# Triangular inversion in a WKV-7 scan: two of three chunk groups keep one factor in the other head's rows, and their products are issued beside those on the diagonal

## The reference, cut to what matters

```
def step(S, inp):
    r_t, w_t, k_t, v_t, a_t, b_t = inp
    sa = jnp.einsum('bhij,bhj->bhi', S, a_t)
    S = S * w_t[:, :, None, :] + sa[..., None] * b_t[:, :, None, :] + v_t[..., None] * k_t[:, :, None, :]
    return S, jnp.einsum('bhij,bhj->bhi', S, r_t)
```

## Time and profile before

| | |
|---|---|
| median of 3 runs | 2486.48 us (2485.86 to 2487.64) |
| the profiled execution | 2485.72 us, its span 2482.9 us |
| busy share of the span | TensorE 88%, VectorE 54%, GpSimd 48%, ScalarE 34% |
| stage B | 546 to some 1135 us |
| the pass looked at | G and N from 787 us, W(0) at 794.80, A at 820.79, next pass's G at 822.20 |

### The profile page before, as it was taken

One profiled execution on the slowest core, in us unless ns is written; L12 is line 12 of the kernel. 1 busy time (PEld: TensorE's weight loads), 2 busy tenths in 40 slices (PEclk: granted clock), 3 DMA queues, 4 the chain that ended last, 5 costly groups with the idle time before them and its releaser, 6 DMA issues.

```text
span 2482.9 us, 57378 instructions
## 1 busy us (share of the span) xinstructions
PE 2190.2 (88%) x22614; PEld 1847.4 (74%) x22614; DVE 1329.2 (54%) x1932; ACT 838.6 (34%) x2187; POOL 1201.1 (48%) x708
## 2 busy tenths in 40 slices
PE   6799999989999999986948989999894999798876
PEld 4698999888888888876948947777693876565655
DVE  6766666664665566655264314454316082548645
ACT  1623323335566656553021223323202111212331
POOL 1266666552233223318847802231583897775234
PEclk8899999999999999996969999999896999899998
DMA  2233334355234323422201210100121221121001
GB/s 88 87 136 145 137 144 166 143 174 96 65 70 88 88 64 69 88 90 78 93 34 69 93 51 35 34 17 34 35 92 71 99 87 43 60 76 60 18 0 68
DMA packets 158909, 197.61 MB, mean 80 GB/s; under 512 B 120992, under 2 KB 123296, under 8 KB 156448
## 3 DMA queue, kind: packets, MB, share of 16 engines
q1 hardware_dynamic: 158752, 195.25, 25.2%
HBM read 156.24 MB, written 38.99 MB: 79 GB/s over the span
## 4 chain that ended last, share of the span: by engine, by line
PE 55%; DVE 8%; issue 7%; ACT 4%; POOL 3%; DVEq 0%; ACTq 0%; POOLq 0%
PE wide L803 8%; PE wide L1233 8%; PE wide L1234 8%; PE wide L1235 8%; PE wide L1710 5%; PE wide L1819 2%; PE wide L818 2%; PE wide L1595 1%; PE wide L1775 1%; PE wide L1803 1%; PE wide L826 1%; PE wide L820 1%; PE wide L2072 1%; POOL x_w L1092 1%; DVE normed L1371 1%
## 5 line engine op out<-in xcount | busy, mean ns | idle before, releaser
L1233 PE MATMUL wide<-mixed_high,w_high_rwkv_in 128*128 128x264 f32 x720 | 212.2, 295 | 29.0 <-ACT log_decay L435 20.1
L1092 POOL TENSOR_TENSOR x_w<-n,masks 128x192 f32<-128x192 f32 x48 | 28.7, 599 | 381.5 <-ACT n L969 381.5
L1235 PE MATMUL wide<-mixed_high,w_low_rwkv_in 128*128 128x264 f32 x720 | 206.6, 287 | 0.0
L1234 PE MATMUL wide<-u_low_second,w_high 128*128 128x512 f32 x464 | 185.5, 400 | 0.0
L1257 POOL TENSOR_TENSOR w_high<-weights,con 128x1024 fp32r<-128x1024 f32 x60 | 147.5, 2458 | 73.7 <-PE wide L1235 63.8
L1350 DVE TENSOR_TENSOR sq_sum<-sq_sum,squares 128x528 f32<-128x528 f32 (+1 forms) x54 | 87.3, 1617 | 178.3 <-ACT squares L1315 178.3
L355 PE MATMUL wide<-mixed_in,weights 128*128 128x264 f32 x672 | 159.1, 395 | 13.3 <-DVE mixed_in L325 12.3
L1233 PEld LDWEIGHTS wide<-mixed_high,w_high_rwkv_in 128*128 128x128 f32 x720 | 138.2, 192 | 37.1 <-ACT log_decay L435 26.3
L1260 POOL TENSOR_TENSOR w_low<-weights,w_high 128x1024 fp32r<-128x1024 f32 x60 | 157.6, 2627 | 4.7
L355 PEld LDWEIGHTS wide<-mixed_in,weights 128*128 128x128 f32 x672 | 129.1, 194 | 40.7 <-issue 9.5
L531 POOL TENSOR_TENSOR w_high_rwkv_in<-weights,con 128x1024 fp32r<-128x1024 f32 x45 | 108.3, 2406 | 71.7 <-PE wide L1235 71.0
(11 more groups left out here) (327 smaller groups left out, 6520.5 us busy)
## 6 DMA issues: line engine op xcount, KB each, us to landing
weights<-in_stream SPq DMA_DIRECT2D x200, 512.0 KB, 3.4
forms<-form SPq DMA_DIRECT2D x16, 2020.5 KB, 6.3
forms_in<-forms SPq DMA_DIRECT2D x96, 144.0 KB, 4.5
forms_in<-forms SPq DMA_DIRECT2D x32, 288.0 KB, 4.4
gate_bonus<-forms SPq DMA_DIRECT2D x16, 576.0 KB, 4.1
r_ahat_r<-forms SPq DMA_DIRECT2D x32, 144.0 KB, 3.5
mixed<-gate_bonus SPq DMA_DIRECT2D x14, 264.0 KB, 2.1
gated<-mixed SPq DMA_DIRECT2D x14, 264.0 KB, 5.0
```

The source lines that it names most:

```text
L1233: pe.matmul(dst, w[0], x[0], start=start, stop=False)
L1234: pe.matmul(dst, w[0], x[1], start=False, stop=False)
L1235: return pe.matmul(dst, w[1], x[0], start=False, stop=stop)
```

## The change

Groups 0 and 1 keep x in the other head's rows, group 2 as before. A product E of groups 0 and 1 then reads one head's rows and writes the other's (cross quadrants), X reads and writes rows of the same head (diagonal), and W is cross again. In group 2 all are diagonal. `side_by_side` issues two products chunk by chunk in turn: E(1) with E(2), X(1) with W(0), X(2) with W(1); then W(2) alone. A W that is paired with an X has TensorE wait for the X of the same group (`x_done`). E(2) is no longer an item of TensorE: the item E(1) issues it, and waits for what both need. On the last level W(1) and W(2) go side by side after a wait for all three copies of E.

```
+        n_other = sbb("n_other_rows", CROSS_GROUPS * GC, C)
...
-        g_mm, n_mm, m_mm, e_mm, xw_mm, a_mm, u_mm, s_mm, y_mm, y_turned = (per_head(n) for n in (
-            "g_mm", "n_mm", "m_mm", "e_mm", "xw_mm", "a_mm", "u_mm", "s_mm", "y_mm", "y_turned"))
+        g_mm, n_mm, m_mm, cross_e_mm, own_e_mm, x_mm, cross_w_mm, own_w_mm, a_mm, u_mm, s_mm, y_mm, y_turned = (per_head(n) for n in (
+            "g_mm", "n_mm", "m_mm", "cross_e_mm", "own_e_mm", "x_mm", "cross_w_mm", "own_w_mm", "a_mm", "u_mm", "s_mm", "y_mm", "y_turned"))
...
-                late = [("E", (0, 0), 3), ("W", 2, 3), ("E", (0, 1), 3), ("E", (0, 2), 3)]
+                late = [("E", (0, 0), 3), ("W", 2, 3), ("E", (0, 1), 3), ("E", (0, 2), 0)]
...
-                        rest += [("E", (lv, g), 3)] if lv else []
+                        rest += [("E", (lv, g), 0 if g == OWN_GROUP else 3)] if lv else []
...
-                    rest += [("XW", (lv, g), 3 if lv == LEVELS - 1 else 6) for g in range(GROUPS)]
+                    rest += [("XW", (lv, g), (3, 3, 0)[g] if lv == LEVELS - 1 else (3, 4, 7)[g]) for g in range(GROUPS)]
...
-            def group(out, lhsT, rhs, chunks, done):
-                chunks = range(NC)[chunks]
-                for n, c in enumerate(chunks):
-                    by_head(out[:, n * C:(n + 1) * C], lhsT(c), rhs(c), True, True, done if n == len(chunks) - 1 else None)
...
+            def x_rows(g):
+                return HEAD_ROWS if g == OWN_GROUP else OTHER_ROWS
+            def one_chunk(product, n):
+                out, out_rows, lhsT, rhs, in_rows, chunks, done = product
+                chunks = range(NC)[chunks]
+                if n < len(chunks):
+                    by_head(out[:, n * C:(n + 1) * C], out_rows, lhsT(chunks[n]), rhs(chunks[n]), in_rows, done if n == len(chunks) - 1 else None)
+            def group(product):
+                for n in range(GC):
+                    one_chunk(product, n)
+            def side_by_side(first, second, ready=None):
+                for n in range(GC + 1):
+                    one_chunk(first, n)
+                    if n == 1 and ready:
+                        wait_heads(pe, *ready)
+                    if n:
+                        one_chunk(second, n - 1)
+            def e_product(lv, g):
+                return (inv_bank[g], x_rows(g), lambda c: n_lvl[:, lv, c, :], of(w), HEAD_ROWS, live(g, lv), e_done(i, lv, g)[0])
+            def x_product(lv, g):
+                return (inv_bank[g], x_rows(g), lambda c: e_all[:, c, :], of(x), x_rows(g), live(g, lv + 1), x_mm)
+            def w_product(lv, g):
+                return (inv_bank[g][:, GC * C:], HEAD_ROWS, of(x), lambda c: e_all[:, c, :], x_rows(g), live(g, lv), w_done(i, lv, g)[0])
...
-                    group(odd_bank[arg % 2], of(x), lambda c: eye[:], grp(arg), w_mm)
+                    group((odd_bank[arg % 2], HEAD_ROWS, of(x), lambda c: eye, x_rows(arg), grp(arg), w_mm))
...
-                    if lv == 0:
-                        pe.wait_ge(q["w_start"], GROUPS * i + g + 1)
-                        pe.wait_ge(q["n_level"], 6 * i + g + 1)
-                        pe.wait_ge(q["b_k_made"], B_K * i + (B_K, B_K - 2, B_K - 1)[g])
+                    if g == OWN_GROUP:
+                        continue
+                    for other in (0,) if g == 0 else (1, OWN_GROUP):
+                        if lv == 0:
+                            pe.wait_ge(q["w_start"], GROUPS * i + other + 1)
+                            pe.wait_ge(q["n_level"], 6 * i + other + 1)
+                            pe.wait_ge(q["b_k_made"], B_K * i + (B_K, B_K - 2, B_K - 1)[other])
+                        else:
+                            pe.wait_ge(q["xw_added"], 15 * i + 3 * (lv - 1) + other + 1)
+                            if lv == 1:
+                                pe.wait_ge(q["n_level"], 6 * i + GROUPS + other + 1)
+                    if g == 0:
+                        group(e_product(lv, 0))
                     else:
-                        pe.wait_ge(q["xw_added"], 15 * i + 3 * (lv - 1) + g + 1)
-                        if lv == 1:
-                            pe.wait_ge(q["n_level"], 6 * i + GROUPS + g + 1)
-                    group(inv_bank[g], lambda c: n_lvl[:, lv, c, :], of(w), live(g, lv), e_mm)
+                        side_by_side(e_product(lv, 1), e_product(lv, OWN_GROUP))
                 elif item == "XW":
                     lv, g = arg
-                    pe.wait_ge(q["e_rows"], 15 * i + 3 * lv + g + 1)
-                    if lv < LEVELS - 1:
-                        group(inv_bank[g], lambda c: e_all[:, c, :], of(x), live(g, lv + 1), None)
-                    group(inv_bank[g][:, GC * C:], of(x), lambda c: e_all[:, c, :], live(g, lv), xw_mm)
+                    last = lv == LEVELS - 1
+                    if not (last and g == OWN_GROUP):
+                        pe.wait_ge(q["e_rows"], 15 * i + 3 * lv + (GROUPS if last and g else g + 1))
+                    if last:
+                        if g == 0:
+                            group(w_product(lv, 0))
+                        elif g == 1:
+                            side_by_side(w_product(lv, 1), w_product(lv, OWN_GROUP))
+                    elif g == 0:
+                        group(x_product(lv, 0))
+                    else:
+                        side_by_side(x_product(lv, g), w_product(lv, g - 1), ready=x_done(i, lv, g - 1))
+                        if g == OWN_GROUP:
+                            group(w_product(lv, g))
...
                     for hd, rows in enumerate(HEAD_ROWS):
                         act.wait_ge(n_mm[hd], GROUPS * i + arg + 1)
                         act.activation(n_all[rows, grp(arg), :], with_rows(hd)[rows, :, 1, :], ACT.Copy).then_inc(q["n_rows"], 1)
+                        if arg != OWN_GROUP:
+                            act.activation(n_other[OTHER_ROWS[hd], grp(arg), :], with_rows(hd)[rows, :, 1, :], ACT.Copy).then_inc(q["n_rows"], 1)
                     for hd in range(2):
                         act.activation(uv[:, par_, hd, grp(arg), :], with_rows(hd)[:, :, 0, :], ACT.Copy).then_inc(q["v_rows"], 1)
...
-                    wait_heads(act, e_mm, 15 * i + 3 * lv + g + 1)
+                    wait_heads(act, *e_done(i, lv, g))
                     act.activation(e_all[:, live(g, lv), :], some(inv_bank[g], live(g, lv)), ACT.Copy).then_inc(q["e_rows"], 1)
...
-                wait_heads(pool, e_mm, 15 * i)
+                wait_heads(pool, cross_e_mm, 10 * i)
+                wait_heads(pool, own_e_mm, 5 * i)
...
-                pool.wait_ge(q["n_rows"], 2 * (GROUPS * i + g + 1))
+                pool.wait_ge(q["n_rows"], n_copies(i, g))
                 x = xw[:, X_OF + par_, flat(g)].rearrange("p (c n) -> p c n", c=GC)
-                pool.tensor_tensor(x, n_all[:, grp(g), :], over_chunks(b_con[:, 0, :]), ALU.mult).then_inc(q["x_start"], 1)
+                n_rows = n_all if g == OWN_GROUP else n_other
+                pool.tensor_tensor(x, n_rows[:, grp(g), :], over_chunks(b_con[:, 0, :]), ALU.mult).then_inc(q["x_start"], 1)
```

More of the change, by code:

```diff
@@ L171, in program @@
         ident, ones, heads = cons("ident", P), cons("ones", P), cons("heads", P)
-        x_loaded, con_loaded = [sem(f"x_or_gate_loaded{k}") for k in range(KD // 2)], sem("con_loaded")
+        x_loaded, con_loaded = [sem(f"x_gate_or_scan_loaded{k}") for k in range(KD // 2)], sem("con_loaded")
         const_set, eps_set = sem("const_set"), sem("eps_set")
@@ L584, in program @@
         LEVELS = 5
+        CROSS_GROUPS, OWN_GROUP = 2, 2
         MASKS = LEVELS + 4
@@ L722, in program @@
         forms_loaded = [q["forms_loaded"], sem("b_forms_loaded1")]
-        scan_loaded = [sem("b_scan_loaded0"), sem("b_scan_loaded1")]
-        gate_loaded = [sem("b_gate_loaded0"), sem("b_gate_loaded1")]
+        gate_loaded, scan_loaded, X_DMA = x_loaded[0:2], x_loaded[2:4], 16
         FORM_DMAS, SCAN_DMAS = 16 * 8, 16 * 3
@@ L731, in wait_scan @@
         def wait_scan(eng, pair, parity):
-            eng.wait_ge(scan_loaded[parity], turn_of(pair, parity, SCAN_DMAS))
+            eng.wait_ge(scan_loaded[parity], X_DMA + turn_of(pair, parity, SCAN_DMAS))
         def wait_gate(eng, pair, parity):
-            eng.wait_ge(gate_loaded[parity], turn_of(pair, parity, 16))
+            eng.wait_ge(gate_loaded[parity], X_DMA + turn_of(pair, parity, 16))
         def is0(i):
@@ L794, in b_k_done, with e_done, w_done, x_done @@
             return 2 * -(-(g + 1) * GC // 2)
+        def e_done(i, lv, g):
+            return (own_e_mm, 5 * i + lv + 1) if g == OWN_GROUP else (cross_e_mm, 10 * i + 2 * lv + g + 1)
+        def w_done(i, lv, g):
+            return (own_w_mm, 5 * i + lv + 1) if g == OWN_GROUP else (cross_w_mm, 10 * i + 2 * lv + g + 1)
+        def x_done(i, lv, g):
+            return x_mm, 12 * i + GROUPS * lv + g + 1
+        def n_copies(i, g):
+            return 10 * i + (4, 8, 10)[g]
         def pe_pass(pe, i, par_, inv, scan, post):
```

(8 more changed lines are left out.)

## The result

The changed kernel takes 2579.5 us (median of 4 runs, 2575.1 to 2582.1), the kernel before in the same rounds 2486.2 us (4 runs, 2485.0 to 2487.6). The ratio is 1.0373, with a 95% interval of 1.0355 to 1.0391: slower by 93 us, where 45 were forecast. The direction held; the size did not.

The account below looks back on a forecast made before the run. It took latency chains through ScalarE and VectorE, close under TensorE's order, to bound the kernel once TensorE is lightened. Copies +1.40 and five segments gave +2.90 us a pass, +45 in all: 2531 us, bounds 2508 to 2555, range with rivals 2498 to 2562.

Parts of the forecast that it names:

- W0 to X0.0: Pass segment from first W to level 0's first X: 4.48 us becoming 5.77, +1.29 us a pass.
- X2.0 to X3.0: Segment from level 2's first X to level 3's: later copies and waits, 5.18 us becoming 5.58, +0.40.
- The copies: N phase: two more ScalarE copies for each of groups 0 and 1, not overlapping, delay N1 and N2: +1.40 us a pass.
- Cross beside diagonal: Levels on TensorE: cross and diagonal products run together, a full level taking 21 chunk steps instead of 27.
- Rival D: Levels: cross and diagonal do not overlap beyond what M does, 1.5 to 3 us more, about 2565; chance 0.10 with Rival C.
- TensorE's waits for itself: Levels: W waits for its group's X, eight a pass, 0 to 0.15 us each; 0.05 taken, inside 1.51 us.
- X2.0's chain: X1.0 to X2.0: square behind w5.0's u copies, then reduction, root and e copy; X2.0 at 5.15 us, +0.39.
- The clock: TensorE's clock over the whole pass: stays at 1.00, adding nothing to the forecast.
- Rival C: Idle TensorE lowers its clock in every pass, 24 to 37 us more, 2561; chance 0.10 with Rival D.
- The joint items: E1 issued with E2, last W pair: waits for both inputs; E01 with E02 starts 4.34 us after W0.
- The order: New places of the walk's half steps and the square: no term of its own, spread over the five level segments.
- 2.85 us a pass off TensorE: Levels: 3.3 us a pass saved by fewer chunk steps, less some 0.45 lost at M and post; swallowed by new waits.

Follow-up runs that it names:

- e1_copies: Kernel before plus only the two more copies of n for groups 0 and 1, made but not read: 2507.1 us, ratio 1.0083.
- e4_pairs: Changed kernel with other pairs, X0, X1, then X2 beside W0, then W1 beside W2: 2586.7 us, ratio 1.0402.
- E30: Not a run: TensorE's item for product E of level 3, group 0.
- e6_dummy: Changed kernel plus 22 products without use ahead of X2.0's wait in passes with a norm: 2563.0 us, ratio 1.0307.
- e10_square_first: Changed kernel with the norm's square one place further up, ahead of w5.0: 2559.8 us, ratio 1.0283.
- e5_split: Changed kernel with the wait for E2's inputs moved between the chunks of the E1 and E2 pair: 2576.5 us, ratio 1.0352.
- e2_order: Kernel before with the change's new item weights only, so new places of the walk's half steps, products and waits as before: 2537.9 us, ratio 1.0206.
- E01: Not a run: product E of level 0, group 1, whose item on TensorE also issues E02 in the changed kernel.
- E02: Not a run: product E of level 0, group 2, its own item before, issued with E01 in the changed kernel.
- e9_unjoined: Changed kernel with before's weights, copies to n_other behind the v copies, and E1, E2 and last level's W as separate items: 2508.6 us, ratio 1.0077.
- e7_late: Changed kernel with n_other copied out of n behind the v copies, so the next N does not wait for it: 2564.0 us, ratio 1.0302.

## Why the prediction was wrong in size and right in direction

The parts of the sum beside the same pass of the two traces, in us:

| part | forecast | measured |
|---|---|---|
| N phase | +1.40 | +1.40 |
| W0 to X0.0 | +1.29 | +1.68 |
| X0.0 to X1.0 | -0.33 | -0.09 |
| X1.0 to X2.0 | +0.39 | +0.69 |
| X2.0 to X3.0 | +0.40 | +1.50 |
| X3.0 to A0 | -0.25 | +0.06 |
| pass | +2.90 | +5.24 |

Over all full passes the mean is +5.76. Pass 0 grew by 7.2 and pass 1 by 2.2, where 2.2 was forecast for each. The prediction trusted its terms to 0.3 us each and let them add up to 1; four of the five came out too low by 0.24 to 0.39, the fifth by 1.10, all of one sign. (Its own bounds add up to 2507 to 2559, not 2508 to 2555; the measured time lies outside both, and outside the 2498 to 2562 that it ended with.)

**The copies: right.** Price, place and the absence of overlap, in the trace and alone in e1_copies.

**Cross beside diagonal: right.** Rival D falls: X and W records alternate, and e4_pairs runs the phase in 1.52 us, where 2.10 was counted before. The Trainium skill (TensorE: Matmul & The Clock Gate, Part 3, The mechanism) has matmuls start in order, first in, first out. Here W0.0's first chunk is issued ahead of X0.1's last, and that chunk's first records (842.95) come ahead of the W chunk's last two (843.02), in other quadrants, as M1's came among E10's in the earlier trace rows; the measurement decides.

**TensorE's waits for itself: the term that was mis-sized.** The prediction took 0.05 us inside 1.51 and named 0.15 each as the upper bound. The gap at 842.76 is 0.18 us from start to start, where the next record of the same quadrant starts 0.05 to 0.06 later without a wait, so some 0.12, near the bound. Two of them make 0.15 of the 0.3 us by which the phase is longer than forecast; the rest has no row. The first W then ended at 1.27 after X0.0 and not at 1.15, and w4.0 began at 3.46, not 3.06. But e4_pairs shows that this size did not decide: with the gaps gone E10 waits for the first add and w4.0 starts no earlier.

**X2.0's chain: right in kind.** The prediction put the square behind the copies of u and X2.0 at 5.15; it came at 5.45 in this pass. The longer X and W phase is 0.17 of this: the copies of u start 2.75 after X1.0, where 2.58 was forecast. It named the wait and did not look at what a stand of 1.3 us does next.

**The clock: the step that failed.** The sum has the clock at nothing, the pass "at clock 1.00"; the runs showed 68.3 us of stage B at 1.2 GHz where before had 3.4. Rival C described it, at 24 to 37 us, and it shared a chance of 0.10 with D. The argument against it was that the full passes stay at 1.00 although their N phases wait. That was an argument from a kernel whose stands are 0.25 to 0.6 us to one that adds stands of 1.1 to 1.7. At these the clock fell in 12 of 14 full passes, so the prediction's own sign of being wrong, PEclk under 1.00, nearly came in every pass. It costs 1.0 us in X2.0 to E30 (3.22 less 2.23), nearly all of the miss of 1.1 in X2.0 to X3.0. The Trainium skill (TensorE: Matmul & The Clock Gate, Part 1, A second HAM failure mode) tells of a kernel that idles briefly between groups and whose clock goes up and down; the trace agrees, with PEclk at 0.50 behind a stand of 1.30 us. e6_dummy, which fills the wait, gives back 16.5 us net; e10_square_first, which removes it, 20, some of them by the wait itself. e6_dummy's gain comes from 37.6 us less at 1.2 GHz. At the same rate the 64.9 us that the changed kernel has more than the one before would cost 28 us, an estimate from these two figures. So the clock is at least 16 us of the 48 missed, perhaps 28, which lies within what rival C gave it. The length of the stand alone does not decide about the fall: it stayed away in passes 3 and 15 of the changed kernel (stands of 1.25 and 1.54 us), in the odd passes of e5_split (1.40), in 10 of 14 passes of e2_order and at N phase stands of up to 1.34 in e1_copies. What else decides is open.

**The joint items: a term that was too small.** E01+E02 was put at 4.34 after W0 and started at 4.78. The copy of w it needs ended at 840.49 (started 840.16, 0.33 long), and TensorE started 0.36 after that, where E02 before started 0.06 behind its copy. The wait's named releaser, `n_levels`, had been made long before, at 837.23. The trace of TensorE's queue shows what lies between: the wait for the copies of w (L945) is passed at 840.53, and two more wait instructions (L946, L947) follow at 840.64 and 840.74, before the first weight load at 840.82, and E01 starts 0.36 us behind the copy in every full pass. Before, E02's wait for its copy sits on its first weight load itself and its other wait is passed early, at 797.34. So a joint item also pays some 0.1 us for each wait instruction that stands behind the last to be fulfilled. In e5_split E01 does not wait for that copy and X0.0 comes 0.47 us earlier. On the last level the item waits for all three copies. Together, e9_unjoined puts the joint items at 26 us, on top of the old order and with 17 us less at 1.2 GHz; in the order of the change their price was not measured alone.

**The order: a term that the sum spread over five segments and never priced by itself.** e2_order has it at 51 us with before's products. The expectation for that kernel was 8 to 24. The prediction put the square's place at 0.39 us of X1.0 to X2.0, where e2_order has +1.07, and gave X2.0 to X3.0 +0.40 for everything, where e2_order has +1.08 with the clock's fall in it. W0 to X0.0 alone, +1.22, it had nearly right (1.29 with the joint item). What lies behind the smaller parts of the 51 us was not taken apart further.

**Where the saving went.** The prediction counted 2.85 us a pass off TensorE and let the new waits swallow it. That they swallow it held; the size of the saving was not measured by itself. In e9_unjoined, which keeps X1 beside W0 and X2 beside W1 and takes away nearly all else that costs, TensorE's busy time is 14 us less and its idle time 35 us more than before. This fits levels that are bound by the loop of product, ScalarE's copy, product and VectorE's add, which a lighter TensorE doesn't shorten; e4_pairs shows it for one place of the loop, the first add, and the rest is argued.

The parts are not to be added: the copies cost 20 us alone and 11 to 16 by their place, the order 51 alone and 29 to 33 when it is taken back, the joint items 26 under the old order. Each depends on the list in which it is measured, and all but the copies' price have some of the clock's in them.

## What to carry to other kernels

An engine that is busy for 98% of a window is not the bound if its queue was laid out to fill other engines' latencies: before making its items fewer, list each item's releaser and ask what fills the latency once the item is gone. Price a change of order by itself, with the old work in it, since it can cost more than the work that it was made for. And where a new wait of a microsecond or more appears on TensorE, price the work behind it at the lower clock too; moving the producer of that wait up by one place in the list was worth 20 us here.

## What the runs showed of the hardware

A stand of 1.30 us in a stretch that is otherwise busy was followed by some 3.4 us at 1.2 GHz (0.50 in the windows above); stands of 1.1 to 1.7 us at this place came with such a fall in 12 of 14 full passes, while the N phase of the same pass, with stands of 1.00 and 0.95 us and other products between them, kept 1.00. Other passes of the runs have a stand of 1.34 us in the N phase, or of 1.40 ahead of X2.0, without a fall. Filling the stand with 22 products without use made the kernel 16.5 us faster.

Four ScalarE copies of 64 partitions each, two of them across the halves, start 0.35 us apart at 0.32 to 0.33 us length, while the copies of 128 partitions behind them overlap (two in 0.55 us). The copies across the halves cost the same as the straight ones. From SBUF to SBUF they took 0.36 us each (e7_late).

Three wait instructions of TensorE behind one another, all fulfilled but the first, passed 0.11 us apart (840.53, 840.64, 840.74), and the first weight load came at 840.82.
